# Products with the zero state, their evictions and the clearing of the states left out in the first chunk of the three branches

## The reference

```python
# RWKV-7, written by token; 8 heads, state 64 x 64 each
S = S * d_t + (S @ a_t) outer b_t + v_t outer k_t ;  y_t = S @ r_t          # S0 = 0
# GLA, chunks of 64 tokens; 4 heads, state 64 x 128 each
o = att @ v_c + (q_c * jnp.exp(b_c)) @ S
S = S * jnp.exp(b_end) + (k_c * jnp.exp(b_end - b_c)).T @ v_c               # S0 = 0
# gated delta rule (GDN), chunks of 64 tokens; 4 heads, state 128 x 128 each
v_new = u_c - w_c @ S          # u = T (v beta), w = T (k beta exp g), T an inverse found by a solve
o = (q_c * jnp.exp(g_c)) @ S + att_c @ v_new
S = S * jnp.exp(g_end) + (k_c * jnp.exp(g_end - g_c)).T @ v_new             # S0 = 0
```

## Time and profile before

| what | value |
|---|---|
| median of 3 runs | 3342.68 us (3339.27 to 3343.28) |
| span of the profiled execution | 3341.7 us |
| TensorE matmul busy | 3125.3 us, 94% |
| TensorE weight load busy | 2416.2 us, 72% |
| VectorE busy | 1803.7 us, 54% |
| ScalarE busy | 708.2 us, 21% |
| mean granted TensorE clock | 0.973 of full |

### The profile page before, as it was taken

How to read it: one execution, slowest core, us unless ns; L and a number is a source line. 1 busy time by engine, 2 the same in 40 slices (tenths; PEclk the granted TensorE clock), 3 DMA queues, 4 the chain that set the end, 5 groups by cost and what they waited for, 6 DMA issues and landing times.

```text
span 3341.7 us, 50848 instructions
## 1 busy us (share of the span) xinstructions
PE 3125.3 (94%) x21694; PEld 2416.2 (72%) x21694; DVE 1803.7 (54%) x2751; ACT 708.2 (21%) x1342; POOL 38.0 (1%) x76
## 2 busy tenths in 40 slices
PE   8999988999998999999889998988999999998998
PEld 8987764558976997765457984544788886465797
DVE  5554554556555555454565555574434562287565
ACT  1112213212112102222311103261211001244110
POOL 1000000000000000000000000000000000000000
PEclk9999999999999999999999999999999999998999
DMA  8654402226655755321215743200223343231352
GB/s 272 227 173 140 164 28 76 76 76 218 213 185 184 252 172 173 128 88 65 88 51 183 236 150 132 76 1 26 76 76 101 114 163 107 77 125 58 127 177 101
DMA packets 279696, 430.75 MB, mean 129 GB/s; under 512 B 9880, under 2 KB 147456, under 8 KB 279472
## 3 DMA queue, kind: packets, MB, share of 16 engines
q1 hardware_dynamic: 273920, 411.52, 36.4%
q0 software_dynamic: 5088, 14.86, 1.4%
q10 hardware_dynamic: 464, 1.12, 0.1%
HBM read 426.43 MB, written 1.05 MB: 128 GB/s over the span
## 4 chain that ended last, share of the span: by engine, by line
PE 82%; DVE 11%; ACT 4%; issue 2%; DMA 1%; DVEq 0%; ACTq 0%; POOL 0%; SPq 0%; PEldq 0%
PE bank L446 80%; PE bank L449 2%; DVE arena L742 1%; ACT xT L993 1%; DVE arena L3700 1%; DVE arena L3621 1%; DVE arena L1761 1%; ACT xT L2810 1%; ACT arena L3137 0%; DMA ring<-in_ffn_w 0%; DVE stats L916 0%; DVE ctok L1773 0%; DMA ring<-in_ple_w_gate 0%; DVE arena L3268 0%; DVE ring L742 0%
## 5 line engine op out<-in xcount | busy, mean ns | idle before, releaser
L446 PE MATMUL bank<-arena 128*128 128x128 f32 (+8 forms) x7068 | 786.7, 286 | 49.9 <-DVEq L3704 8.4
L446 PE MATMUL bank<-xT,ring 128*128 128x128 f32 (+3 forms) x4640 | 808.5, 335 | 20.5 <-ACTq L2818 9.9
L446 PEld LDWEIGHTS bank<-arena 128*128 128x128 f32 (+3 forms) x7068 | 667.7, 164 | 165.9 <-issue 27.0
L446 PEld LDWEIGHTS bank<-xT,ring 128*128 128x128 f32 (+1 forms) x4640 | 691.9, 194 | 130.7 <-issue 55.0
L446 PE MATMUL bank<-ring,xT 128*128 128x512 f32 (+2 forms) x1408 | 592.2, 572 | 17.0 <-ACT xT L2810 8.7
L446 PEld LDWEIGHTS bank<-ring,xT 128*128 128x128 f32 x1408 | 261.2, 194 | 287.6 <-issue 268.7
L446 PE MATMUL bank<-ring,arena 128*128 128x256 f32 (+1 forms) x1584 | 448.5, 436 | 19.7 <-DVE arena L839 6.5
L446 PEld LDWEIGHTS bank<-ring,arena 128*128 128x128 f32 x1584 | 302.8, 193 | 140.2 <-issue 91.0
L782 DVE TENSOR_TENSOR arena<-arena,bank 128x256 f32<-128x256 f32 (+1 forms) x198 | 92.2, 466 | 427.1 <-PE bank L446 287.2
L694 ACT COPY arena<-bank 128x256 f32<-128x256 f32 (+1 forms) x264 | 107.8, 408 | 777.5 <-PE bank L446 776.5
L742 DVE TENSOR_TENSOR arena<-ring,arena 128x1024 f32<-128x1024 f32 (+1 forms) x216 | 257.1, 1190 | 7.4
(11 more groups left out here) (391 smaller groups left out, 2140.1 us busy)
## 6 DMA issues: line engine op xcount, KB each, us to landing
ring<-in_ffn_w SPq DMA_DIRECT2D x88, 1024.0 KB, 8.0
ring<-in_w_in SPq DMA_DIRECT2D x32, 2048.0 KB, 7.7
ring<-in_ffn_w_in SPq DMA_DIRECT2D x44, 1024.0 KB, 6.9
arena<-in_ada_w SPq DMA_DIRECT2D x18, 2048.0 KB, 13.6
ring<-in_ffn_w SPq DMA_DIRECT2D x16, 2048.0 KB, 7.9
ring<-in_ffn_w_out SPq DMA_DIRECT2D x12, 2048.0 KB, 8.2
ring<-in_hgrn_w_in SPq DMA_DIRECT2D x12, 2048.0 KB, 7.9
ring<-in_ffn_w SPq DMA_DIRECT2D x8, 1536.0 KB, 6.6
```

The lines of the kernel that those rows point to most:

```text
L446: return self.e.matmul(o, lhsT, rhs, start=start, stop=stop, skip_group_check=True)
```

## The change

In the first chunk of each branch, and only there:

- RWKV: the 8 state products of (1) and the 8 of (3) are not issued, and the value products begin the accumulation themselves. `Hst` is not cleared. The first update is one instruction, the addition's bank times the decay, in place of an add and a multiply. TensorE no longer waits for `state_ready` before the first chunk.
- GLA: the 4 state products are not issued, `gS` is not cleared, and the first update is one copy out of the bank in place of two instructions.
- GDN: keys x state and queries x state are not issued, so two banks fewer pass through the ring. `dX` is a copy of `dv_tok` (from SBUF to SBUF) in place of four instructions that read the bank; VectorE now waits for `own_rows_clear` before it, which ScalarE raises by 2 instead of 1. L2431 is left out, L2449 becomes a copy, the four instructions of L2461 become one copy of 128x512, `dSt` is not cleared, and TensorE does not wait for `state_ready`; its first work after the solve is the gate step.

The diff (twelve columns of indentation taken off):

```diff
--- before.py
+++ after.py
@@ -1629,10 +1629,7 @@
-v.memset(Hst[:], 0.0).then_inc(dve_step, dve.up(dve_step))
-dve.wait_ge(dve_step, dve.sent(dve_step))
 dve.sem_inc(v_tok_ready, dve.up(v_tok_ready))
-dve.sem_inc(state_ready, dve.up(state_ready))
@@ -1674,11 +1671,17 @@
-        v.tensor_tensor(Hst[:], bank[:, 0:256].rearrange("p (a n) -> p a n", a=4), Hst[:],
-                                         ALU.add).then_inc(to_dve.freed, dve.up(to_dve.freed))
+        e = P * tt + 64 * c + 63
+        decay = eL[:, :, e:e + 1].broadcast_to([P, 4, 64])
+        added = bank[:, 0:256].rearrange("p (a n) -> p a n", a=4)
+        if tt == c == 0:
+            v.tensor_tensor(Hst[:], added, decay, ALU.mult).then_inc(to_dve.freed, dve.up(to_dve.freed))
+            dve.wait_ge(to_dve.freed, dve.sent(to_dve.freed))
+            dve.sem_inc(state_ready, dve.up(state_ready))
+            continue
+        v.tensor_tensor(Hst[:], added, Hst[:], ALU.add).then_inc(to_dve.freed, dve.up(to_dve.freed))
         dve.wait_ge(to_dve.freed, dve.sent(to_dve.freed))
-        e = P * tt + 64 * c + 63
-        ins = v.tensor_tensor(Hst[:], Hst[:], eL[:, :, e:e + 1].broadcast_to([P, 4, 64]), ALU.mult)
+        ins = v.tensor_tensor(Hst[:], Hst[:], decay, ALU.mult)
         ins.then_inc(state_ready, dve.up(state_ready))
         dve.wait_ge(state_ready, dve.sent(state_ready))
@@ -1894,14 +1897,16 @@
-        pe.wait_ge(state_ready, pe.due(state_ready))
+        if tt or c:
+            pe.wait_ge(state_ready, pe.due(state_ready))
...
         for h in range(8):
             hp, par = h // 2, h % 2
             o = bank[r_, h * 64:(h + 1) * 64]
-            pe.mm(o, AR[:, par, hp, ct], Hst[:, hp], True, False)
-            mm = pe.mm(o, M4[:, h, 0], v_own[tt][c][:, h * 64:(h + 1) * 64], False, True)
+            if tt or c:
+                pe.mm(o, AR[:, par, hp, ct], Hst[:, hp], True, False)
+            mm = pe.mm(o, M4[:, h, 0], v_own[tt][c][:, h * 64:(h + 1) * 64], tt == c == 0, True)
             if h == 7:
                 mm.then_inc(to_dve.filled, 1)
...
@@ -1919,8 +1924,9 @@
-            pe.mm(o, AR[:, 2 + par, hp, ct], Hst[:, hp], True, False)
-            pe.mm(o, M4[:, h, 1], v_own[tt][c][:, h * 64:(h + 1) * 64], False, False)
+            if tt or c:
+                pe.mm(o, AR[:, 2 + par, hp, ct], Hst[:, hp], True, False)
+            pe.mm(o, M4[:, h, 1], v_own[tt][c][:, h * 64:(h + 1) * 64], tt == c == 0, False)
             mm = pe.mm(o, M4[:, h, 3], SAs[c][:, h * 64:(h + 1) * 64], False, True)
...
@@ -2012,8 +2018,6 @@
 v.memset(gQb[:], 0.0).then_inc(dve_step, dve.up(dve_step))
-dve.wait_ge(dve_step, dve.sent(dve_step))
-v.memset(gS[:], 0.0).then_inc(dve_step, dve.up(dve_step))
 dve.wait_ge(dve_step, dve.sent(dve_step))
 dve.wait_ge(gk_log_ready, dve.due(gk_log_ready))
@@ -2088,7 +2092,11 @@
-        for hp in range(2):
+        if tt == c == 0:
+            ins = v.tensor_copy(gS[:], bank[:, 0:2 * P].rearrange("p (a n) -> p a n", a=2))
+            ins.then_inc(to_dve.freed, dve.up(to_dve.freed))
+            dve.wait_ge(to_dve.freed, dve.sent(to_dve.freed))
+        for hp in range(2) if tt or c else ():
             ins = v.scalar_tensor_tensor(out=gS[:, hp], in0=gS[:, hp], scalar=gE[:, hp * SEQ + e:hp * SEQ + e + 1],
                                          in1=bank[:, hp * P:(hp + 1) * P], op0=ALU.mult, op1=ALU.add)
...
@@ -2173,8 +2181,9 @@
-            pe.mm(o, gatt[:, par, 2 * tt + hp], gv_own[tt][c][:, h * P:(h + 1) * P], True, False)
-            mm = pe.mm(o, gQb[:, par, o0:o0 + 64], gS[:, hp], False, True)
+            mm = pe.mm(o, gatt[:, par, 2 * tt + hp], gv_own[tt][c][:, h * P:(h + 1) * P], True, tt == c == 0)
+            if tt or c:
+                mm = pe.mm(o, gQb[:, par, o0:o0 + 64], gS[:, hp], False, True)
@@ -2247,7 +2256,7 @@
 for c in range(2):
     act_clear(act, dX[c], c)
     act_clear(act, dvn[c], c)
-act.sem_inc(own_rows_clear, act.up(own_rows_clear))
+act.sem_inc(own_rows_clear, act.up(own_rows_clear, 2))
@@ -2401,16 +2410,19 @@
 for tt in range(2):
     dve_solve_start(dve, dU[:, 4 * tt:4 * tt + 4], dAT[:, tt])
-v.memset(dSt[:], 0.0).then_inc(dve_step, dve.up(dve_step))
-dve.wait_ge(dve_step, dve.sent(dve_step))
 dve_solve(dve, lambda b: dAT[:, b], dT, dU, dAm)
-dve.sem_inc(state_ready, dve.up(state_ready))
 for tt in range(2):
     for c in range(2):
         r_ = slice(64 * c, 64 * c + 64)
-        dve.wait_ge(to_dve.filled, to_dve.next_filled())
-        bank = to_dve.filled_bank()
-        for h in range(4):
+        first = tt == c == 0
+        if first:
+            dve.wait_ge(own_rows_clear, dve.due(own_rows_clear, 2))
+            v.tensor_copy(dX[c][r_], dv_tok[r_, tt]).then_inc(dve_step, dve.up(dve_step))
+            dve.wait_ge(dve_step, dve.sent(dve_step))
+        else:
+            dve.wait_ge(to_dve.filled, to_dve.next_filled())
+            bank = to_dve.filled_bank()
+        for h in () if first else range(4):
             s_ = slice(h * P, (h + 1) * P)
             ins = v.scalar_tensor_tensor(out=dX[c][r_, s_], in0=bank[r_, s_],
                                          scalar=nbe_s[r_, 4 * tt + h:4 * tt + h + 1], in1=dv_tok[r_, tt, s_],
...
@@ -2426,12 +2438,13 @@
-        dve.wait_ge(to_dve.filled, to_dve.next_filled())
-        bank = to_dve.filled_bank()
-        v.tensor_tensor(y3, bank[r_, :].rearrange("p (h n) -> p h n", h=4),
-                                         eG_s[r_, 4 * tt:4 * tt + 4].unsqueeze(2).broadcast_to([64, 4, P]),
-                                         ALU.mult).then_inc(to_dve.freed, dve.up(to_dve.freed))
-        dve.wait_ge(to_dve.freed, dve.sent(to_dve.freed))
+        if not first:
+            dve.wait_ge(to_dve.filled, to_dve.next_filled())
+            bank = to_dve.filled_bank()
+            v.tensor_tensor(y3, bank[r_, :].rearrange("p (h n) -> p h n", h=4),
+                            eG_s[r_, 4 * tt:4 * tt + 4].unsqueeze(2).broadcast_to([64, 4, P]),
+                            ALU.mult).then_inc(to_dve.freed, dve.up(to_dve.freed))
+            dve.wait_ge(to_dve.freed, dve.sent(to_dve.freed))
         dve.wait_ge(to_dve.filled, to_dve.next_filled())
         bank = to_dve.filled_bank()
         v.tensor_copy(dvn[c][r_], bank[r_, :]).then_inc(dve_step, dve.up(dve_step))
@@ -2446,7 +2459,10 @@
-        ins = v.tensor_tensor(br_tok[r_, tt], bank[r_, :], br_tok[r_, tt], ALU.add)
+        if first:
+            ins = v.tensor_copy(br_tok[r_, tt], bank[r_, :])
+        else:
+            ins = v.tensor_tensor(br_tok[r_, tt], bank[r_, :], br_tok[r_, tt], ALU.add)
@@ -2456,7 +2472,11 @@
-        for h in range(4):
+        if first:
+            ins = v.tensor_copy(dSt[:], bank[:].rearrange("p (h n) -> p h n", h=4))
+            ins.then_inc(to_dve.freed, dve.up(to_dve.freed))
+            dve.wait_ge(to_dve.freed, dve.sent(to_dve.freed))
+        for h in () if first else range(4):
             o = (4 * tt + h) * 2 + c
             ins = v.scalar_tensor_tensor(out=dSt[:, h], in0=dSt[:, h], scalar=eend_s[:, o:o + 1],
                                          in1=bank[:, h * P:(h + 1) * P], op0=ALU.mult, op1=ALU.add)
@@ -2524,7 +2544,7 @@
 pe_solve(pe, dT, dU, dAm, dPm)
-pe.wait_ge(own_rows_clear, pe.due(own_rows_clear))
+pe.wait_ge(own_rows_clear, pe.due(own_rows_clear, 2))
 blk = pe.block()
@@ -2532,8 +2552,9 @@
-        pe.wait_ge(state_ready, pe.due(state_ready))
-        for t0 in (4, 0):
+        if tt or c:
+            pe.wait_ge(state_ready, pe.due(state_ready))
+        for t0 in (4, 0) if tt or c else ():
             pe.wait_ge(to_dve.freed, to_dve.next_free())
             bank = to_dve.free_bank()
             for h in range(4):
```

## The result

The changed kernel takes 3323.76 us (median of 4 runs, 3319.94 to 3327.46) against 3341.25 us (4 runs, 3339.27 to 3343.28): the ratio is 0.9945, 95% interval 0.9931 to 0.996. That is 17.5 us less. The profiled execution spans 3325.7 us; its own time is 3327.46 us, the longest of the four.

A forecast was written before the change was run, and what follows sets the result against it. TensorE was taken as the bound, with 82% of the span. RWKV 1.87, GLA 1.18 and GDN 2.05 sum to 5.10 us a layer, 10.2 for two, giving 3332.5 us; range 3327.5 to 3338.

The forecast's parts named there:

- RWKV's products: RWKV's first chunk: dropping 16 of 32 records and 16 of 48 readout records saves 0.93 + 0.94 us a layer.
- the burst's mean: RWKV readout: mean price over 80 weight loads, 0.048 us a record, 0.77 us for 16; taken as lower bound.
- GDN: 2.00 + 0.05 forecast: GDN's first chunk: `dU x dX` starts 2.00 us earlier, and the state copy leaves 0.05 us; 2.05 us a layer.
- the bracket: GDN after the solve: gate step starts 0.12 to 0.41 us after VectorE's end, so `dU x dX` 1.86 to 2.15 earlier.
- Rival A: GDN after the solve: step gives nothing, something unseen such as the weight block holds TensorE; 3336.6 us, chance 0.14.
- The covers: First state updates of RWKV and GDN: TensorE's gate steps hide VectorE's savings of 0.46 and 0.81 us.
- rival B: First state updates of RWKV (0.46 us) and GDN (0.81) were on the path after all; 3330.0 us, chance 0.10.
- The clearings: The three state clearings on VectorE: each hidden by a wait for another engine, the largest 0.48 us; worth 0.
- The rest of the kernel shifts unchanged: Code outside the changed chunks: later weight loads move up with the work, so the 10.2 us saved reach the end.
- The allowance: Half-clock spells outside the chunks: 1.1 us shift for each layer's rest and the stages behind, some 3 us either way.
- Rival C: Later in the kernel: the gain is given back at a fixed wait, such as a transfer; 3342.7 us, chance 0.05.
- Rival D: Recurrence chunks: fewer products drop TensorE's clock, a full spell costing 3.35 us; six spells give 3352.6 us, chance 0.03.

The follow-up runs named there:

- either set: Changed kernel plus unread 128x512 products, either in the four transitions without ada products or before RWKV's second solve and after GLA's last product: 3321.56 and 3323.49 us.

## Why the prediction was wrong

- RWKV's products: 0.93 and 0.94 us forecast, 1.87 measured. Right, with 0.94 and not the burst's mean for the readout.
- GLA: 1.18 forecast, 1.20 measured.
- GDN: 2.00 + 0.05 forecast, 2.31 measured. The gate step started at the early end of the bracket, 0.12 us after VectorE (2.16 up to `dU x dX`), and 0.15 us came behind it. Rival A is refuted: nothing else held TensorE after the solve. The mechanism stood; for two layers the middle of the bracket was 0.3 us too low, and 0.2 came behind `dU x dX`.
- The covers over the updates of RWKV and GDN held (rival B's mechanism is refuted; its time came nearer than mine for another reason).
- **The clearings: "Worth 0" was a term put at nothing, and wrong for one of three.** The prediction read the one of `dSt`, where VectorE idled 1.82 us afterwards, and took the others for the same pattern. The clearing of `Hst` stands ahead of the raise of `v_tok_ready`, and TensorE waits for it: 0.31 us a layer, 0.6 in all, shown by putting it back alone. Together with GDN the direct sum becomes 5.69 us a layer, 11.4 in place of 10.2. By itself that would have given about 3331 us, inside the range: it is not what took the time out of it.
- **"The rest of the kernel shifts unchanged" is the step that failed.** In the medians 5.7 to 6.1 us lie beyond the direct sum, where "some 3 us in all" were allowed either way. In the profiles (the second of each kernel) they are half-clock spells: 176.9 us of half-clock time before, 156.0 in the changed kernel, with 3.3 us off the stretch from 1169 us, 1.3 off the one from 1507, 1.5 off those from 2053 and 1.2 off the last row of the table, 1.5 given back at 1940. Over all stretches and kernels a microsecond at half clock costs about 0.3 us, where the stretch from 1169 us, with TensorE busy throughout its spell, lost 0.5 (3.3 for 6.8). That many spells lie where TensorE waits anyway would explain it and is not shown.
- The price of one spell was sized right: 6.8 us of half clock less shorten the stretch from 1169 us by 3.3 us (the forecast said at most 3.35). The allowance was not. It was taken from one pair of stretches, 97.99 and 96.89 us, which differ by 3.4 us of half clock and so by 1.1 us, and counted about three times. The table has seven stretches that change, and a single one, that from 1169 us, uses up all of the 3 us.
- The range's lower end was reckoned wrongly too: half a spell, 1.7 us, beyond rival B's 3330.0 is 3328.3 us and not 3327.5. The measured 3323.76 lies below both.
- Rival C, the gain given back at a fixed wait, is refuted by the 17.5 us at the end. Rival D is refuted: the changed chunks run at the full clock and no spell entered them.

The Trainium skill, "TensorE: Matmul & The Clock Gate", Part 1, says of the products at the lower clock ahead of the rise that their number varies from run to run and that this penalty is under 1% of a typical span. The excess here, 5.7 of 3340 us, is 0.2% and agrees in size, and the executions of one kernel do vary, by 10 us. But the changed kernel came out 5.5 to 6.1 us beyond its direct sum in four comparisons, with and without added work, and that is more than a draw from run to run gives.

What stays open: why this kernel drew +5.7. Displacing the unchanged code by one product took out the same two spells, near 989 and 1385 us, and layer 1's stretches from 1940 us follow layer 1's own distances; but more than one part comes with an excess, the branches do not add, and no run here predicts it for a new kernel. That the spells are the place of the excess is shown by the stretches; that they fall as they do by a rule that could have been applied beforehand is not.

## What to carry to other kernels

When a TensorE-bound program has spells of half clock, shortening or lengthening it can redraw some of those behind it, as one product of 0.86 us did here: give a small change a range of at least the largest few spells in either sign, and judge a 2 us edit by its own stretch, not by the end. A clearing is hidden only if nothing behind it in its queue raises a semaphore that the bounding engine waits for; look at that raise for each one. And the spells themselves are a target: 24 unread products at idle places, all of them together, gave 12 us, as much as the whole change did directly; either set alone gave nothing that the medians show.

## What was not expected of the hardware

- The pattern of spells can survive a displacement. The changed kernel with 0, 5.1 and 11.1 us of added work has the same stretches to about 0.2 us from 1014 to 2792 us (1767.5 to 1768.0 us in four profiles), so the clock's falls follow the program there and not the time since its start. It does not always: with only the clearing of `Hst` back, 0.31 us a layer, the same part took 1764.7 us in the one profile.
- The clock can fall with TensorE busy: in five profiles it fell 2.2 to 2.7 us into a run of 8-column products, and the traces show no idle time of TensorE for over 100 us before.
- Either set of unread products alone left the median where it was (3321.56 and 3323.49 us); both sets gave more than their sum (3310.67).
- VectorE copies 64x512 elements between two places of on-chip memory in 0.42 us (L2420) and out of a bank in 0.68 us (L2463). The Trainium skill, "VectorE: DVE Perf Modes", What auto-detection actually checks, ties the doubled rate to a single source with source and destination in SBUF; by that rule the copy out of a bank stays at the single rate, and the trace agrees in direction, with 0.68 against 0.42 us for the same size.
